# A two-layer transformer block kernel on one Trainium2 core: stick-breaking scores kept in PSUM, and the first expert's tile 0 ahead of the router's logits

## The reference

```python
def stick_breaking_attention(q, k, v):
    z = jnp.einsum('bqhd,bshd->bhqs', qb, k).astype(jnp.float32) * scale
    mask = kpos[None, :] < t[:, None]
    log_1m = jnp.where(mask, jax.nn.log_sigmoid(-z), 0.0)
    between = lax.cumsum(log_1m, axis=3, reverse=True) - log_1m
    w = jnp.where(mask, jnp.exp(jax.nn.log_sigmoid(z) + between), 0.0)
    o = jnp.einsum('bhqs,bshd->bqhd', w.astype(v.dtype), v)

def hierarchical_moe(x, w_grp, b_grp, w_rt, b_rt, w_gate, w_up, w_down):
    # group by argmax of x @ w_grp + b_grp, two experts in it by top-k, 16 experts:
    # sum over experts of combine * (silu(x @ w_gate) * (x @ w_up)) @ w_down
```

## Time and profile before

| | |
|---|---|
| median of 3 runs (lowest, highest) | 1394.05 us (1392.94, 1397.39) |
| the profiled execution | 1392.4 us, of which the span is 1390.3 |
| TensorE busy | 1338.6 us (96%) |
| VectorE, ScalarE busy | 1073.5 us (77%), 626.5 us (45%) |
| chain that ended last | PE 78%, DVE 15%, ACT 4% |
| DMA, 860 to 1030 us | 0.79 to 0.88 busy in stretches of 40 or 50 us |
| weight load requests near the gathers of the first MoE | one at 841.30, the next at 861.25 |
| split of the `up` weights of expert 1, first MoE | L2050, starts at 841.83, 2.29 us |
| L2792, L2794, first MoE, tile 0 | 0.41 and 0.42 us, the second starts at 846.93 |

### The profile page before, as it was taken

The page is one execution under the profiler, slowest core; times in us unless marked ns, Lnnn a source line. Parts: engine busy times, 40 slices in busy tenths (PEclk is TensorE's granted clock), DMA queues, the critical chain, the costliest instruction groups (busy, mean ns, idle before and its releaser), DMA issues.

```text
span 1390.3 us, 22503 instructions
## 1 busy us (share of the span) xinstructions
PE 1338.6 (96%) x9046; PEld 1197.7 (86%) x9046; DVE 1073.5 (77%) x1408; ACT 626.5 (45%) x891; POOL 61.2 (4%) x90
## 2 busy tenths in 40 slices
PE   7999999998999999999999999999999979999997
PEld 6999888997999988998898688888879957888886
DVE  7788798667887889747878886687887588768786
ACT  4543432334433332333313854566651286556663
POOL 1110100003000000000200300000000000000000
PEclk9999999999999999999999999999999999999999
DMA  8544744544454543542854042788865504378791
GB/s 266 160 161 148 249 147 152 175 159 136 128 176 152 194 143 119 182 152 101 259 182 152 2 152 96 267 297 279 297 217 186 178 31 150 114 257 308 266 314 77
DMA packets 195062, 249.63 MB, mean 180 GB/s; under 512 B 5850, under 2 KB 168922, under 8 KB 194960
## 3 DMA queue, kind: packets, MB, share of 16 engines
q1 hardware_dynamic: 189200, 227.66, 49.2%
q0 software_dynamic: 5072, 18.73, 3.7%
q10 hardware_dynamic: 688, 1.82, 0.3%
HBM read 246.09 MB, written 2.10 MB: 179 GB/s over the span
## 4 chain that ended last, share of the span: by engine, by line
PE 78%; DVE 15%; ACT 4%; issue 2%; DMA 1%; POOL 1%; SPq 0%; DVEq 0%; ACTq 0%; POOLq 0%
PE bank L515 36%; PE bank L547 8%; PE bank L1155 7%; PE bank L769 4%; PE bank L1214 4%; DVE wL L2050 4%; PE bank L1192 4%; PE bank L601 2%; DVE wH L2048 2%; DVE proj L2228 1%; PE bank L649 1%; PE bank L478 1%; ACT proj L2018 1%; PE bank L1236 1%; PE bank L1060 1%
## 5 line engine op out<-in xcount | busy, mean ns | idle before, releaser
L515 PE MATMUL bank<-hH,wH 128*128 128x256 f32 x1624 | 470.3, 290 | 9.5 <-DVE wL L2050 6.6
L515 PE MATMUL bank<-hL,wH 128*128 128x256 f32 x1624 | 459.9, 283 | 0.0
L515 PE MATMUL bank<-hH,wL 128*128 128x256 f32 x1488 | 421.4, 283 | 0.0
L2050 DVE TENSOR_TENSOR wL<-ring,wH 128x2048 fp32r<-128x2048 f32 x156 | 357.0, 2292 | 39.7 <-ACT wH L1872 22.6
L515 PEld LDWEIGHTS bank<-hH,wH 128*128 128x128 f32 x1624 | 311.6, 192 | 18.4 <-DVE wL L2050 9.7
L515 PEld LDWEIGHTS bank<-hL,wH 128*128 128x128 f32 x1624 | 311.9, 192 | 1.4 <-issue 0.2
L515 PEld LDWEIGHTS bank<-hH,wL 128*128 128x128 f32 x1488 | 285.8, 192 | 0.0
L1872 ACT ACTIVATE wH<-ring 128x2048 fp32r<-128x2048 f32 x53 | 101.8, 1921 | 15.8 <-PE bank L547 10.1
L1595 ACT ACTIVATE big<-bank 128x512 f32<-128x512 f32 x40 | 23.9, 597 | 148.2 <-PE bank L515 148.1
L2048 DVE CAST wH<-ring 128x2048 fp32r<-128x2048 f32 x53 | 65.2, 1229 | 12.9 <-PE bank L515 10.4
L2422 DVE SCALAR_TENSOR_TENSOR L<-big,bank 128x512 f32<-128x512 f32 x32 | 22.0, 687 | 51.4 <-PE bank L769 51.2
(11 more groups left out here) (505 smaller groups left out, 2490.6 us busy)
## 6 DMA issues: line engine op xcount, KB each, us to landing
ring<-in_w_gate SPq DMA_DIRECT2D x40, 1024.0 KB, 5.2
ring<-in_w_in SPq DMA_DIRECT2D x34, 1024.0 KB, 5.3
ring<-in_moe_w_down SPq DMA_DIRECT2D x29, 1024.0 KB, 5.4
ring<-in_moe_w_gate SPq DMA_DIRECT2D x27, 512.0 KB, 4.6
ring<-in_moe_w_up SPq DMA_DIRECT2D x27, 512.0 KB, 5.6
ring<-in_sb_w_in SPq DMA_DIRECT2D x9, 1024.0 KB, 5.2
ring<-in_w_out SPq DMA_DIRECT2D x8, 1024.0 KB, 5.0
ring<-in_ab_w_in SPq DMA_DIRECT2D x8, 1024.0 KB, 5.6
```

The costliest lines, as they stand in the source:

```text
L515: last = mm(ps[:, m * CW:m * CW + (width if token_major else S)], a, b, start=k == 0 and i == 0, stop=k == KT - 1 and i == 2)
L2050: tt(low, raw_w, high, ALU.subtract).then_inc(split_ready, 1)
```

## The change

The masks of the scores are added in PSUM: for each head one more product, the identity `maskR[:, 0]` by a mask in `maskR[:, 1:3]`. The prefix sums, with matrices `negs` that hold `tri` and `ones` times -1, are added into the same bank as the scores, so a head holds one bank from its scores to its last Exp, and the banks `sc2` go. VectorE's addition becomes a bitwise AND of the scores read as integers, from PSUM (|z|); the subtraction goes; the softplus operation reads the scores from PSUM. ScalarE's Abs goes, and its last Exp reads PSUM and writes `sbw`. `maskR` and `negs` are made by three VectorE instructions at the end of the first MoE. In both MoE stages the two instructions for expert 0's tile 0 stand in front of the logits.

```diff
@@ sb_qk, sb_cum, sb_pv (TensorE)
-                        if s == T - 1:
-                            last.then_inc(*fills(("sz2", h + a)))
+                           SQT[r0:r0 + HD, ct * S + s * P:(ct + 1) * S], start=s == 0, stop=False, skip_group_check=True)
+                if h == 0:
+                    eng.wait_ge(mask_made, 2)
+                for a in range(2):
+                    two = both[a][:, :].rearrange("p (s n) -> p s n", s=T)[:, :, 0:P]
+                    mm(two, maskR[:, 0, :], maskR[:, 1:3, :], start=False, stop=True, skip_group_check=True).then_inc(scores_made, 1)
...
+                eng.wait_ge(mask_made, 3)
                 sp = spb[h % 4]
-                ps = open_bank(eng, ("sc2", h))
-                mm(ps[:, 0:S], tri, sp[:, 0:S], start=True, stop=False)
-                mm(ps[:, P:S], ones[:, :], sp[:, S:S + P], start=False, stop=True)
-                mm(ps[:, S:S + P], tri, sp[:, S:S + P], start=True, stop=True).then_inc(*fills(("sc2", h)))
+                ps = banks[items[("sz2", h)][0]]
+                mm(ps[:, 0:S], negs[:, 0:P], sp[:, 0:S], start=False, stop=False, skip_group_check=True)
+                mm(ps[:, P:S], negs[:, P:2 * P], sp[:, S:S + P], start=False, stop=False, skip_group_check=True)
+                mm(ps[:, S:S + P], negs[:, 0:P], sp[:, S:S + P], start=False, stop=True, skip_group_check=True)\
+                    .then_inc(*fills(("sz2", h)))
...
-                    eng.wait_ge(w_ready, nth(pe, w_ready))
+                    eng.wait_ge(*emptied_at(("sz2", h + a)))
@@ ScalarE
-                    eng.wait_ge(*emptied_at(("sc2", i - 3)))
-                    a = sbw[(i - 3) % 8]
-                    act(a, a, ACT.Exp).then_inc(w_ready, 1)
+                    h = i - 3
+                    eng.wait_ge(*filled_at(("sz2", h)))
+                    act(sbw[h % 8], banks[items[("sz2", h)][0]][:, 0:S + P], ACT.Exp).then_inc(*empties(("sz2", h)))
...
-                    eng.wait_ge(*emptied_at(("sz2", i)))
-                    act(sp, sbw[i % 8], ACT.Abs).then_inc(se_done, 1)
+                    eng.wait_ge(abs_made, nth(ac, abs_made))
@@ VectorE, MoE
+                first_hidden(0)
                 eng.wait_ge(*filled_at(("rt", l)))
...
-                for t in range(T):
-                    h, ps = sth[t], banks[items[("gu", l, 0, t)][0]]
...
+                first_hidden(1)
...
+                if l == 0:
+                    v.tensor_copy(maskR[:, 1:3, :], sbmask[:, 0:P].unsqueeze(1).to_broadcast([P, 2, P])).then_inc(mask_made, 1)
+                    ts(negs[:, 0:P], tri, -1.0, None, ALU.mult)
+                    ts(negs[:, P:2 * P], ones[:, :], -1.0, None, ALU.mult).then_inc(mask_made, 1)
                 layer_norm(ffn(l), 2 * l + 1, *((("xT", 1), split_no["sv2", 0, 1]) if l + 1 < DEPTH else ()))
@@ VectorE, stick-breaking
-                    tt(sbw[h % 8], sbw[h % 8], ps[:, 0:S + P], ALU.subtract).then_inc(*empties(("sc2", h)))
...
-                    tt(sbw[i % 8], ps[:, 0:S + P], sbmask, ALU.add).then_inc(*empties(("sz2", i)))
...
+                    if i >= 4:
+                        eng.wait_ge(*filled_at(("sz2", i - 4)))
+                    eng.wait_ge(scores_made, nth(ve, scores_made))
+                    ps = banks[items[("sz2", i)][0]][:, 0:S + P]
+                    ts(spb[i % 4].bitcast(I32), ps.bitcast(I32), 0x7FFFFFFF, None, ALU.bitwise_and).then_inc(abs_made, 1)
...
-                    stt(spb[h % 4], sbw[h % 8], 0.0, spb[h % 4], ALU.max, ALU.add).then_inc(sp_ready, 1)
+                    stt(spb[h % 4], banks[items[("sz2", h)][0]][:, 0:S + P], 0.0, spb[h % 4], ALU.max, ALU.add).then_inc(sp_ready, 1)
```

More of the change, by code:

```diff
@@ L110, in build @@
         PT, = beneath(("PT", [P, 2, T, S]))
+        negs, = beneath(("negs", [P, 2 * P]))
         hsR = sb("hsR", [P, 2, 2, HID_], F32R)
@@ L238, in build @@
             sem, ("late_loaded", "roped", "trig_arg", "trig_done", "gelu_arg", "gelu_tanh", "gelu_done"))
[L239 to L240 removed]
+        gelu_bias, ln_rstd, cl_max, cl_exp, cl_ready, sp_ln, sp_ready = map(
+            sem, ("gelu_bias", "ln_rstd", "cl_max", "cl_exp", "cl_ready", "sp_ln",
                   "sp_ready"))
@@ L1298, in sb_qk @@
                         r0 = a * HD
-                        last = mm(both[a][:, s * S:S + s * P], SKT[r0:r0 + HD, ct * S + s * P:ct * S + (s + 1) * P],
-                                  SQT[r0:r0 + HD, ct * S + s * P:(ct + 1) * S], start=True, stop=True)
-                        if s == T - 1:
-                            last.then_inc(*fills(("sz2", h + a)))
+                        mm(both[a][:, s * S:S + s * P], SKT[r0:r0 + HD, ct * S + s * P:ct * S + (s + 1) * P],
+                           SQT[r0:r0 + HD, ct * S + s * P:(ct + 1) * S], start=s == 0, stop=False, skip_group_check=True)
[4 more added lines that the diff above has]
+                    mm(two, maskR[:, 0, :], maskR[:, 1:3, :], start=False, stop=True, skip_group_check=True).then_inc(scores_made, 1)
             def sb_cum(h):
                 eng.wait_ge(sp_ready, nth(pe, sp_ready))
+                eng.wait_ge(mask_made, 3)
                 sp = spb[h % 4]
-                ps = open_bank(eng, ("sc2", h))
-                mm(ps[:, 0:S], tri, sp[:, 0:S], start=True, stop=False)
-                mm(ps[:, P:S], ones[:, :], sp[:, S:S + P], start=False, stop=True)
-                mm(ps[:, S:S + P], tri, sp[:, S:S + P], start=True, stop=True).then_inc(*fills(("sc2", h)))
+                ps = banks[items[("sz2", h)][0]]
[3 more added lines that the diff above has]
+                    .then_inc(*fills(("sz2", h)))
             def sb_pv(h):
                 for a in range(2):
-                    eng.wait_ge(w_ready, nth(pe, w_ready))
+                    eng.wait_ge(*emptied_at(("sz2", h + a)))
                 if h % 8 == 0:
@@ L2729, in first_max, with first_hidden @@
                     eng.wait_ge(done, own(done))
+                def first_hidden(t):
+                    h, ps = sth[t], banks[items[("gu", l, 0, t)][0]]
+                    eng.wait_ge(*filled_at(("gu", l, 0, t)))
+                    eng.wait_ge(g_tanh, nth(ve, g_tanh))
+                    stt(h, h, 1.0, ps[:, 0:HID], ALU.add, ALU.mult).then_inc(ve_done, 1)
+                    eng.wait_ge(ve_done, own(ve_done))
+                    tt(h, h, ps[:, HID:2 * HID], ALU.mult).then_inc(*empties(("gu", l, 0, t)))
+                first_hidden(0)
                 eng.wait_ge(*filled_at(("rt", l)))
@@ L2919, in _ @@
             for i in range(SB_H + 3):
[L2920 to L2924, removed]
[L2925 to L2934 removed]
+                if i < SB_H:
+                    if i >= 4:
[3 more added lines that the diff above has]
+                    ts(spb[i % 4].bitcast(I32), ps.bitcast(I32), 0x7FFFFFFF, None, ALU.bitwise_and).then_inc(abs_made, 1)
+                    eng.wait_ge(abs_made, own(abs_made))
                 if 1 <= i < SB_H + 1:
```

7 lines of the change are left out of this document (3 added, 4 removed).

## The result

The changed kernel took 1384.6 us (median of 6 runs, 1382.31 to 1387.97), the kernel before 1392.99 (6 runs). The ratio is 0.9924, 95% interval 0.9903 to 0.9944: faster by 0.8%, inside the forecast range and 1.4 us above the forecast. The profiled execution of the changed kernel took 1382.38 us, its span is 1380.6, 9.7 less than before. The runs of one kernel lie mostly in two groups some 5 us apart (here 1382.3 to 1382.9 and 1386.3 to 1388.0), so small differences are read from stages of the traces.

A forecast was written before the change was run, and what follows sets the result against it. TensorE, busy 1338.6 of 1390.3 us, was taken as the bound, so only its waits and slow clock pay. Terms -6.5 - 4.4 - 0.6 + 0.7 = -10.8 gave 1381.6 profiled, 1383.2 median; range 1380 to 1388.

The forecast's parts named there:

- The loop: Stick-breaking stage: waits through VectorE and TensorE set the pace, 4.23 us a pair against 4.62; 3.3 us gained.
- (b): Rival, stick-breaking stage: pace of the pair unchanged at 4.62 us, only start and tail gain; 1386.5 us, chance 0.12.
- Start and tail: Stick-breaking stage, before pair 4 and after pair 14: 1.0 us gained at the start, 2.2 at the tail.
- The magnitude: Stick-breaking stage: VectorE's abs reading PSUM takes 0.56 us; 0.53 by the skill's table.
- First expert: Both MoE stages, tile 0 ahead of the logits: 4.4 us gained in the first, 0.6 in the second.
- part 1: Stick-breaking stage, scores stay in PSUM: 6.5 us gained.
- The masks: End of the first MoE: three VectorE instructions making maskR and negs lose 0.7 us, between 0.5 and 1.0.
- The risk named for the clock: End of first MoE: after TensorE's wait of 1.6 us the clock might fall, costing up to another 1.6.
- (a): Rival, stick-breaking stage: the loop is shorter, in the limit ScalarE's 3.5 us bounds the pair; 1379.5 us, chance 0.13.
- (c): Rival, pulled-forward MoE: weights don't arrive 4.4 us sooner, gain given back; 1387.6 us, chance 0.10 together with (e).
- (d): Rival, stick-breaking stage: integer bitwise operation in PSUM is slow, kernel slower than before; chance 0.04.
- (e): Rival, first MoE: the bank isn't the one, the 2.80 us wait stays; 1387.6 us, chance 0.10 together with (c).

The follow-up runs named there:

- mask_twice: Changed kernel with each mask product made twice; 1383.61 us, one run.
- mask_first: Changed kernel with a pair's two mask products ahead of its scores in the same bank; 1383.2 us.
- part2_only: Kernel before with only the first expert's tile 0 finished ahead of the logits in both MoE stages; 1387.64 us.
- part1_only: Changed kernel with the first expert's tile 0 put back behind the selection matrices; 1390.23 us.
- three: Changed kernel with scores ahead of the values product, masks made late in VectorE's idle time, and mask products ahead of the scores; 1379.43 us.
- scores_first: Changed kernel with the scores of a later pair put ahead of the values product in TensorE's queue; 1380.44 us.
- masks_late: Changed kernel with the three mask-making instructions moved into VectorE's idle time ahead of the first magnitude; 1387.09 us.
- abs_twice: Changed kernel with each magnitude taken twice on VectorE; 1391.81 us, one run.
- before_scores_first: Kernel before with a pair's scores put ahead of the values product of an earlier pair; 1393.15 us.
- both: Changed kernel with scores ahead of the values product and masks made late in VectorE's idle time; 1379.74 us.

## Why the prediction was right, and where it was off

**Time.** 1383.2 forecast, 1384.6 measured; in the profiled execution 1381.6 against 1382.4. That is closer than the terms deserve, and partly luck: the stick-breaking stage fell 1.6 short, the slow clock behind the masks took 0.3 that was not in the sum, the others gave some 0.8 back, 0.26 of it where nothing was edited, and 0.3 of the gain lies outside the span.

**The loop.** Its shape and four of its links were read off rows and hold: 0.59, 0.61, 1.08 and 0.80 (1120.10, 1120.69, 1121.30, 1122.38, 1123.18). The fifth, scores to magnitude, was put at 0.96 + 0.19 = 1.15 and is 1.35. The 0.19 was to pay for two more passes and the mask product; together they take 0.39. The mask product costs 0.11 of its own (mask_twice). The other 0.28 is the two passes, the second head's last score product, which the magnitude did not wait for before, and the change from 64-row to 128-row weights, for which the sum had no term; no run parts these two. mask_first, with neither between scores and magnitude, gives 1.03. The period of 4.43 lies as near to rival (b)'s 4.62 as to the forecast's 4.23. So five periods gave 24.46 - 22.17 = 2.3 us and not 3.3 (22.17 = 1133.38 - 1111.21, the magnitudes of heads 14 and 4).

**Start and tail.** Start: I counted 4 x 0.12 = 0.5 us for four mask products; between the first scores of the pair 0 and those of pair 4 lie 9.79 us, 8.93 before, so 0.86, twice the 0.43 that two mask products take when scores follow. From the scores to the magnitude 1.37 instead of 1.1. Gain 0.4 instead of 1.0. The tail is 6.83 where 6.8 was worked out, 2.2 gained, as said. Rows of the changed kernel, TensorE and VectorE:

```profile
1100.05 0.93 PE L1300 MATMUL bank<-big 64*128 64x256 f32 x8
1100.90 0.50 PE L1306 MATMUL bank<-maskR 128*128 128x256 f32 x2
1101.33 0.70 PE L1300 MATMUL bank<-big 64*128 64x256 f32 x4
...
1109.84 0.92 PE L1300 MATMUL bank<-big 64*128 64x256 f32 x8
...
1133.38 0.56 DVE L2937 TENSOR_SCALAR proj<-bank 128x384 int32<-128x384 int32 x1 [1.03 <-PE bank L1306]
...
1140.21 0.50 PE L548 MATMUL bank<-wH,hH 128*128 128x512 f32 x1
```

Together with the tail 0.4 + 2.3 + 2.2 = 4.9 of the forecast 6.5 (1100.05 to 1140.21 is 40.16; 45.04 before).

**The magnitude.** 0.557 us, as assumed (0.56). The rule of the Trainium skill (VectorE: DVE Perf Modes, "Why PSUM operands drop a tier") that an operand in PSUM brings no double rate fits: reading PSUM the AND takes as long as the softplus beside it (558 ns), which has two tensor inputs. No run has the AND from SBUF to compare. The estimate of 0.53 from that page's table is 0.03 short of this row.

**First expert.** 4.4 forecast, 4.32 in part2_only; 0.6 for the second MoE, 0.72. The further 0.27 of the second MoE comes with part 1, from the weight chunk that is no longer late (part1_only); the prediction had no term for it.

**The masks.** 0.7 forecast; 0.47 for the instructions, and a lower clock for 0.28 more in some executions. The risk named for the clock came true, at a sixth of the 1.6 feared: TensorE is idle for 0.6 of the 4 us there at the full clock (3.39 busy) and for 0.3 at the lower one, so part of the slower products fills time in which it waited anyway.

**Rivals.** (a) would have needed ScalarE's 3.5 us a pair. It was further off than its chance of 0.13 says: TensorE's products alone take 3.84 us a pair where it runs without a gap (three), and 4.03 with one more change of shape (scores_first). The prediction never added them up. (b), (c), (d) and (e) did not occur: (e) is excluded by the gathers at 850.13, (c) by the first MoE as a whole (3.85 us shorter), (b) by the 4.43, (d) by the 557 ns.

## What to carry over

When a step moves from one engine to another, draw the loop of waits that is left, but also add up each engine's own queue for one period: the loop gives the pace, the fullest queue says how much a reordering can still bring (here a loop of 4.43 us a pair, and queues of 4.03 and 3.84 with four and three changes of weight shape; the new order changes the queue's own sum). A product added behind a group is priced by what stands ahead of it in the queue, and by whether its weights have another shape than its neighbours'; put products of one weight shape side by side. Small preparations belong in a stretch in which their engine waits anyway, here 8.8 us ahead of the first magnitude, and not in the chain to a layer norm.

## What the runs showed of the hardware

*A lower clock while TensorE is busy.* Stretches of masks_late (profiled execution 1387.49 us) and of the changed kernel (1382.38) at the same place, far ahead of everything that the edits touch:

```profile
140.00:160.00 20.00, 20.00 (x121) 16.21 (x120) 11.95 (x16) 5.09 (x11) 3.76 (x6) 0.83 0.44 150
```

```profile
140.00:160.00 20.00, 20.00 (x145) 16.74 (x145) 13.11 (x18) 6.71 (x16) 4.28 (x6) 1.00 0.45 156
```

TensorE is busy in both, at a mean clock of 0.83 in the first, with 121 products in place of 145. The same work comes in masks_late 1.4 us later than in the changed kernel at 22 us, 4.3 at 162 and 5.9 at 756; from 740 to 760 its clock is 0.93. part2_only and abs_twice have the lower clock in the same two stretches, before_scores_first has it from 140 to 160 and from 720 to 740 (0.91), both from 740 to 760 alone (0.83). Which execution gets which was not found.

*The clock after a pause.* TensorE's wait of 1.40 to 1.41 us ahead of the transposes was followed by 1.2 GHz in four profiles (changed kernel, scores_first, mask_first, abs_twice) and not in two (part1_only, mask_twice). After the wait of 0.93 or 0.94 (before, part2_only, masks_late, before_scores_first, both, three) it stayed at 2.4 GHz in all six.

*A change of weight shape* between consecutive products costs TensorE 0.18 us (three against scores_first) to 0.21 (mask_first), though its record shows it busy all the time: a TensorE that looks full can still be made shorter.
